# A two-block layer stack on one core: the second block's branch gates by seven products, as fillers of its attention

## The reference, cut to what matters

```python
proj = h @ w_in
(dq, dk, dv, sq, sk, sv, mq, mk, mv, g_diff, g_sb, g_moba) = jnp.split(proj, offsets, axis=-1)
...
merged = (jax.nn.sigmoid(g_diff) * (a_out @ w_diff_o)
          + jax.nn.sigmoid(g_sb) * (b_out @ w_sb_o)
          + jax.nn.sigmoid(g_moba) * (c_out @ w_moba_o))
return merged @ w_out
```

## Time and profile before

| | |
|---|---|
| median of 3 runs | 3370.44 us (3370.26 to 3370.8) |
| profiled execution | 3372.12 us, its span 3370.2 us |
| PE busy | 3293.4 us (98%), 22634 records |
| PEld busy | 2943.6 us (87%) |
| DVE busy | 2117.7 us (63%) |
| ACT busy | 683.3 us (20%) |
| POOL busy | 187.2 us (6%) |

### The profile page before, as it was taken

One profiled execution on the slowest core, in us unless ns is written; L12 is line 12 of the kernel. 1 busy time (PEld: TensorE's weight loads), 2 busy tenths in 40 slices (PEclk: granted clock), 3 DMA queues, 4 the chain that ended last, 5 costly groups with the idle time before them and its releaser, 6 DMA issues.

```text
span 3370.2 us, 54290 instructions
## 1 busy us (share of the span) xinstructions
PE 3293.4 (98%) x22634; PEld 2943.6 (87%) x22634; DVE 2117.7 (63%) x4269; ACT 683.3 (20%) x1675; POOL 187.2 (6%) x140
## 2 busy tenths in 40 slices
PE   7999999999999999999999999999999999999999
PEld 5888755788888888878999999987999999978999
DVE  3579554456554157765799685744586886644685
ACT  2101442012211011142122111124211212032211
POOL 0000000005443400000000000000000000000000
PEclk9999999999999999999999999999999999999999
DMA  6243001223223433403544445632444444633443
GB/s 235 81 174 127 26 26 63 96 85 128 87 86 111 147 152 129 175 35 113 199 179 168 169 163 176 175 138 100 147 169 169 163 165 159 193 115 121 155 163 126
DMA packets 67396, 453.76 MB, mean 135 GB/s; under 512 B 7376, under 2 KB 11856, under 8 KB 15056
## 3 DMA queue, kind: packets, MB, share of 16 engines
q1 hardware_dynamic: 66384, 446.09, 37.3%
q10 hardware_dynamic: 768, 4.20, 0.7%
HBM read 445.02 MB, written 1.05 MB: 132 GB/s over the span
## 4 chain that ended last, share of the span: by engine, by line
PE 88%; DVE 7%; ACT 2%; DMA 1%; issue 1%; SPq 0%; DVEq 0%; ACTq 0%
PE bank L1353 62%; PE bank L1041 14%; DVE conv_sum L2848 3%; PE bank L1667 2%; PE bank L1153 1%; PE bank L1183 1%; PE bank L1106 1%; PE bank L1091 1%; PE bank L1208 1%; PE bank L1714 1%; PE bank L1298 1%; DMA weight_ring<-w_o 1%; PE bank L1503 0%; PE bank L1276 0%; DMA weight_ring<-w_ada 0%
## 5 line engine op out<-in xcount | busy, mean ns | idle before, releaser
L1353 PE MATMUL bank<-normed,weight_ring 128*128 128x128 f32 (+1 forms) x5472 | 764.1, 295 | 5.3 <-ACT normed L1884 1.5
L1353 PEld LDWEIGHTS bank<-normed,weight_ring 128*128 128x128 f32 x5472 | 706.8, 192 | 42.5 <-issue 8.0
L1353 PE MATMUL bank<-normed,mixer_small 128*128 128x128 f32 (+1 forms) x3040 | 387.2, 281 | 0.0
L1353 PEld LDWEIGHTS bank<-normed,mixer_small 128*128 128x128 f32 x3040 | 366.4, 192 | 4.9
L1353 PE MATMUL bank<-region_a,weight_ring 128*128 128x128 f32 (+1 forms) x2128 | 294.4, 293 | 0.6 <-DVE region_a L2805 0.6
L1353 PEld LDWEIGHTS bank<-region_a,weight_ring 128*128 128x128 f32 x2128 | 272.1, 192 | 11.7 <-issue 2.0
L1353 PE MATMUL bank<-turned,weight_ring 128*128 128x256 f32 (+1 forms) x944 | 199.0, 353 | 0.0
L1353 PEld LDWEIGHTS bank<-turned,weight_ring 128*128 128x128 f32 x944 | 163.6, 190 | 18.4
L1041 PE MATMUL bank<-turned,weight_ring 128*128 128x256 f32 x768 | 179.5, 382 | 0.0
L1041 PEld LDWEIGHTS bank<-turned,weight_ring 128*128 128x128 f32 x768 | 140.8, 190 | 24.2 <-issue 6.9
L1353 PE MATMUL bank<-region_a,mixer_small 128*128 128x128 f32 (+1 forms) x1232 | 161.8, 282 | 0.0
(11 more groups left out here) (340 smaller groups left out, 4883.5 us busy)
## 6 DMA issues: line engine op xcount, KB each, us to landing
weight_ring<-w_ada SPq DMA_DIRECT2D x48, 1024.0 KB, 5.6
weight_ring<-w_up SPq DMA_DIRECT2D x44, 1024.0 KB, 4.8
weight_ring<-w_f1up SPq DMA_DIRECT2D x44, 1024.0 KB, 4.8
weight_ring<-w_f2up SPq DMA_DIRECT2D x44, 1024.0 KB, 4.8
weight_ring<-w_gt SPq DMA_DIRECT2D x32, 1024.0 KB, 4.8
weight_ring<-w_qk SPq DMA_DIRECT2D x24, 1024.0 KB, 4.8
weight_ring<-w_v SPq DMA_DIRECT2D x20, 1024.0 KB, 5.4
weight_ring<-w_pj SPq DMA_DIRECT2D x16, 1024.0 KB, 4.8
```

The costliest lines, as they stand in the source:

```text
L1353: mm = nc.tensor.matmul(bank[u.bank][:, pair.columns(p)], lhs(k), rhs(k), start=begins and p in pair.opens and k == 0, stop=ends and p in ...
```

## The change

The 24 gate tiles become 12 pairs, computed by the seven products. `GATE_PARTS` cuts a pair's products over its four filler halves: 1 and 2, then 7 and 6, in the even place; 5, then 3 and 4, in the odd place. Bank 6 holds y, bank 7 holds x. VectorE makes the four differences of the normed tokens ahead of the loop (into the free half of `normed`), the weight sums of pair j at n = 2j - 2 (`gate_sums`), and the mixes of tile n - 1 at n (`gate_mix`); the order in its loop at n is finish, scores, exponent, mix, sums (n even), store, squares. ScalarE copies only product 1 of a pair (`gate_first`, 128 columns). Sums have semaphores of their own (`gsums_made`, `gsums_used`); the second feed-forward part's first sums wait for the last of them.

```diff
+GATE_PARTS = [(1, 2), (7, 6), (5,), (3, 4)]
...
-                waited = 0 if 4 in order else 4
+                waited = had if had is not None else 0 if 4 in order else 4
...
+                    if name == "gt2":
+                        x = 2 * (g % 2) + half
+                        if g == 0 and half == 0:
+                            pe.wait_ge(turned_ready, T.next(turned_ready, 4))
+                        seven(b, g // 2 % SUM_RING, plan.pairs[name][g // 2], KD // 2, gate_act, gsums_made, gsums_used,
+                              True, True, l, wsum, None, None, GATE_PARTS[x], (0, 0, 3, 3)[x])
+                        return
...
-                    else:
-                        mm = product(bank[u.bank][:, 0:SEQ], b, g % 2 * KD + half * n, hnorm2, 0, SEQ, n, half * n,
-                                     half == 0, half == 1)
...
-                    a_(gates2[g // KD][:, g % KD, :], bank[u.bank][:, 0:SEQ], ACT.Copy).then_inc(bank_free[u.bank], 1)
+                    a_(one_gate[:, g // 2 % 2, :], bank[units[g].bank][:, 0:P], ACT.Copy).then_inc(one_copied, 1)
...
+                def gate_sums(j):
+                    ...
+                    if at_ >= SUM_RING:
+                        dve.wait_ge(gsums_used, at_ - SUM_RING + 1)
+                    dve.wait_ge(slot_landed[b.slot], (count(b, 0, l) + 1) * 16)
+                    ...
+                    v.tensor_tensor(s1, a21, a22, ALU.add).then_inc(gsums_made, 1)
+                    V.sent(gsums_made)
+                    v.tensor_tensor(a21, a11, a21, ALU.subtract).then_inc(gsums_made, 1)
+                    V.sent(gsums_made)
+                    dve.wait_ge(gsums_made, V.made["gsums_made"] - 1)
+                    v.tensor_tensor(s2, s1, a11, ALU.subtract).then_inc(gsums_made, 1)
+                    dve.wait_ge(gsums_made, V.at(gsums_made, V.sent(gsums_made)))
+                    v.tensor_tensor(s4, a12, s2, ALU.subtract).then_inc(gsums_made, 1)
+                    V.sent(gsums_made)
+
+                def gate_mix(n):
+                    ...
+                    if n % 2 == 0:
+                        mix_y(g // 2, y, gate_tiles(g), one_gate)
+                    else:
+                        mix_x(y, x, gate_tiles(g))
...
                     if 16 <= n + 1 < 24:
                         exponent(n + 1)
+                    gate_mix(n - 1)
+                    if n % 2 == 0:
+                        gate_sums(n // 2 + 1)
                     if n >= 1 and n % 2 == 0:
                         store(n // 2 - 1)
...
+                gate_mix(23)
                 store(11)
```

More of the change, by code:

```diff
@@ L272, in filler2 @@
         self.blocks[name][-1].after = self.units[name][-1]
+        if name == "gt2" and g % 2:
+            self.pairs.setdefault(name, []).append(Pair(self.units[name][-2:], P, False))
     def take_blocks(self, name, dram, n, cols, first=0):
@@ L1318, in attention1, with seven @@
                         turn(n + 1)
-            def seven(b, s, pair, n, act, made, used, begins, ends, l=0, ring=wsum, midway=None, behind_first=None, part=None):
+            def seven(b, s, pair, n, act, made, used, begins, ends, l=0, ring=wsum, midway=None, behind_first=None, part=None, had=None):
                 def quarter(q):
@@ L1677, in layer2 @@
                         value_part(u, b, t, range(KD)).then_inc(bank_full[u.bank], 1)
+                gate_act = Halves(hnorm2, lambda k: hn[:, k, 0:P], lambda k: hn[:, 4 + k, 0:P], lambda k: hn[:, k, P:2 * P],
+                                  0, KD // 2, 0, P, lambda what, k: None, lambda k: hn[:, 4 + k, P:2 * P])
                 def filler_half(i, half):
@@ L1686, in filler_half @@
                     n = KD // 2
-                    if name == "sv2":
-                        mm = value_part(u, b, g % 2, range(half * n, half * n + n))
-                    else:
-                        mm = product(bank[u.bank][:, 0:SEQ], b, g % 2 * KD + half * n, hnorm2, 0, SEQ, n, half * n,
-                                     half == 0, half == 1)
+                    mm = value_part(u, b, g % 2, range(half * n, half * n + n))
                     if half:
@@ L2882, in sums_of @@
                         dve.wait_ge(sums_used, V.next(sums_used))
+                    if x == FFN2:
+                        dve.wait_ge(gsums_used, (l + 1) * 12)
                     dve.wait_ge(slot_landed[b.slot], (count(b, 0, l) + 1) * 16)
@@ L3256, in halves, with mix_y @@
                     V.sent(turned_ready)
-                def mix_y(j, y, dst):
+                def mix_y(j, y, dst, one=one2):
                     dve.wait_ge(one_copied, V.next(one_copied))
@@ L3263, in mix_y @@
                     v.tensor_tensor(seg[:, 0:2], bank[y.bank][:, P:3 * P].rearrange("p (s c) -> p s c", c=P),
-                                    one2[:, j % 2, :].unsqueeze(1).to_broadcast([P, 2, P]), ALU.add).then_inc(mix_step, 1)
+                                    one[:, j % 2, :].unsqueeze(1).to_broadcast([P, 2, P]), ALU.add).then_inc(mix_step, 1)
                     dve.wait_ge(mix_step, V.at(mix_step, V.sent(mix_step)))
@@ L3446, in layer2 @@
                         dve.wait_ge(rope_ready, V.at(rope_ready, V.made["rope_ready"]))
+                n = KD // 2
+                b11, b21 = hnorm2[:, 0:n, 0:P], hnorm2[:, n:KD, 0:P]
+                b12, b22 = hnorm2[:, 0:n, P:2 * P], hnorm2[:, n:KD, P:2 * P]
+                dve.wait_ge(hnorm2_ready, (l + 1) * KD // 2)
+                v.tensor_tensor(hn[:, 0:n, 0:P], b12, b11, ALU.subtract).then_inc(turned_ready, 1)
+                dve.wait_ge(turned_ready, V.sent(turned_ready))
+                v.tensor_tensor(hn[:, n:KD, 0:P], b22, hn[:, 0:n, 0:P], ALU.subtract).then_inc(turned_ready, 1)
@@ new lines, in layer2, with gate_tiles @@
+                second = V.sent(turned_ready)
+                v.tensor_tensor(hn[:, n:KD, P:2 * P], b22, b12, ALU.subtract).then_inc(turned_ready, 1)
+                V.sent(turned_ready)
+                dve.wait_ge(turned_ready, second)
+                v.tensor_tensor(hn[:, 0:n, P:2 * P], b21, hn[:, n:KD, 0:P], ALU.subtract).then_inc(turned_ready, 1)
+                V.sent(turned_ready)
+                def gate_tiles(g):
+                    return gates2[g // KD][:, g % KD:g % KD + 2, :].rearrange("p a c -> p (a c)")
@@ new lines, in gate_sums @@
+                def gate_sums(j):
+                    if j >= 12:
+                        return
+                    b, at_ = plan.blocks["gt2"][j], 12 * l + j
+                    if j == 0:
+                        full_bank(plan.units["qk2"][-1], 0, l)
+                    if at_ >= SUM_RING:
+                        dve.wait_ge(gsums_used, at_ - SUM_RING + 1)
+                    dve.wait_ge(slot_landed[b.slot], (count(b, 0, l) + 1) * 16)
+                    a11, a12, a21, a22 = (ring_t[:, b.slot * SLOT + q * (KD // 2 * P):b.slot * SLOT + (q + 1) * (KD // 2 * P)] for q in range(4))
+                    s1, s2, s4 = (wsum[:, j % SUM_RING, i, 0:KD // 2 * P] for i in range(3))
+                    v.tensor_tensor(s1, a21, a22, ALU.add).then_inc(gsums_made, 1)
[7 more added lines that the diff above has]
+                    V.sent(gsums_made)
@@ L3448, in scores @@
+                def gate_mix(n):
+                    g = n if n % 2 == 0 else n - 1
+                    if not 0 <= g < 24:
+                        return
+                    y, x = plan.units["gt2"][g:g + 2]
+                    if n % 2 == 0:
+                        mix_y(g // 2, y, gate_tiles(g), one_gate)
+                    else:
+                        mix_x(y, x, gate_tiles(g))
                 def scores(n):
```

14 lines of the change are left out of this document (9 added, 5 removed).

## The result

The changed kernel takes 3405.93 us (median of five executions, 3399.0 to 3408.24) against 3370.44 us of five of the kernel before beside it (3365.01 to 3373.39): 1.0107 times, 95% interval 1.0093 to 1.012. The direction is the forecast's; the time is 12.5 us over it, at the upper edge of the range. The profiled execution took 3407.5 us, its span 3405.7.

What follows compares the result with a forecast made beforehand. TensorE was taken as the bound (88% of the chain of waits). New waits of +19.3 us a layer less a gain of 7.8 give +11.5, +23.0 over two layers: 3393.4 us from the median 3370.44, range 3374 to 3406.

Steps and rivals of the forecast that it cites:

- The gain: Gate products on TensorE: a pair goes from 6.91 to 6.25 us, saving 7.8 us a layer, 15.6 in all.
- The rule that weight loads set the pace: TensorE's gate records: loads alone would take a pair from 6.91 to 12.1 us, kernel some 3495 us; chance 0.01.
- The waits: TensorE waiting for VectorE's queue in the attention stage: 21.85 us a layer against 2.6 before, so +19.3.
- turn 8: TensorE's weight turn at n = 8, VectorE late from earlier periods: wait 2.2 us, bounds 0.8 and 3.6.
- turn 10: TensorE's weight turn at n = 10: VectorE's path 5.77 us against TensorE's 5.00, wait 0.8.
- norm sums at n = 10, 12: TensorE's norm sums, behind VectorE's sums, store and squares: 5.71 us against 4.01, wait 1.7, twice.
- turns 12, 14: TensorE's weight turns that waited 1.25 us for the norm's way through ScalarE: the half between shrinks, so 2.1, twice.
- turn 16: TensorE's weight turn at n = 16: VectorE's path 6.07 us against TensorE's 5.00, wait 1.05.
- turns 18, 20, 22 with product 5: TensorE's last three even-head turns: VectorE done 6.97 us after the odd turn against 3.66, wait 3.3, partly before product 5.
- the rival of a falling clock: TensorE's clock falls behind the new waits: six periods at 3.3 us each, kernel 3413 us; chance 0.04.
- TensorE stays the bound and the sums hide: Rival: VectorE's sums cost TensorE nothing in the attention stage, kernel 3354.8 us, faster; chance 0.08.
- Only the last stretch waits: Rival: VectorE catches up at n under 16, leaving 2.4 us a layer, kernel 3375.2, no measurable difference; chance 0.08.

Runs made afterwards that it cites:

- e8: Changed kernel with e5's order (mix before exponent, halves reordered, sums in odd places), each pair's sums one period earlier: 3358.3 us, ratio 0.9968.
- e9: Changed kernel with unused matmuls on TensorE ahead of turns 8, 12, 14, 16, 18, 20, 22 and the norm sums, 38 a layer: 3391.49 us, ratio 1.0068.
- e7: Changed kernel with six unused 256-column matmuls on TensorE ahead of each of the turns 18, 20 and 22: 3394.31 us, ratio 1.0085.
- e5: Changed kernel reordered: sums in odd places, mix before exponent, a pair's second half as products 3 and 4, then 5: 3361.86 us, ratio 0.9978.
- e1: Changed kernel without the gates' weight sums on VectorE, products taking raw weight blocks: 3366.52 us, ratio 0.9998.
- e2: Changed kernel with the same sums moved from even places behind the x mix to odd places behind the y mix: 3371.6 us, ratio 1.001.
- e3: Changed kernel with two of the four weight sums left in the even place and two moved to the odd: 3380.56 us, ratio 1.0029.
- e4: Kernel before, with five more VectorE instructions of 512 columns in each of places 16, 18 and 20: 3389.77 us, ratio 1.0069.

## Why the forecast was right in its waits and wrong in its time

**The gain** held. Sixteen records take 1.89 us with the change of kind (2305.70 to 2307.59 in the changed kernel; 1.79 + 0.1 forecast). In e8 the stage less its waits (3.85 us in six, each some 0.16 more from start to start, as 2310.60 + 0.99 to 2314.55 is 2.96 for a row of 2.79) is 117.1 us; before, 127.28 less 2.6 and twice 0.16 is 124.4. That is 7.3 a layer, the forecast 7.8. The rule that weight loads set the pace, which would have given 3495 us, does not hold here: PEld is busy 106.92 of 121.90 us in e8 and the records still keep their pace.

**The waits** held one by one. Forecast, then the row of layer 1 (a row lacks the 0.16):

| place | forecast | profiled idle |
|---|---|---|
| turn 8 | 2.2 | 1.99 |
| turn 10 | 0.8 | 0.70 |
| norm sums at n = 10, 12 | 1.7, 1.7 | 1.53, 1.54 |
| turns 12, 14 | 2.1, 2.1 | 2.09, 2.15 |
| turn 16 | 1.05 | 0.99 |
| turns 18, 20, 22 with product 5 | 3.3 each | 2.79 + 0.18 each |
| product 5 at n = 23 | 0.3 | 0.18 |

Turn 8's wait, the least certain of them, came the way that was forecast: from the second period on VectorE's sums start 8.93 us apart (2232.76, 2241.69, 2250.62), where 9.0 was forecast, against TensorE's 8.29 (8.3 forecast). e9 puts the waits in one number: 139.15 us where 138.8 was forecast.

**The step that failed** is the clock. The forecast took TensorE's clock as 1.00 in and behind the new waits, so its sum has no term for it, and gave the rival of a falling clock 0.04, with the reason that the kernel before's waits of 1.25 us left the stage's clock at 1.00. That row was about waits of 1.25 us and was carried to waits of 3.3 us. The clock did fall behind the long waits of both layers, for 7.8 us a layer (e9). The rival had the mechanism and the place, and was too dear: it priced six periods at 3.3 us each, where e7 gives 2.5; its 3413 against 3405.93. It should have had a larger part of the chance, or the forecast's own range a term of 0 to 20 us for it.

The trace of the kernel before could have said so. Its attention stages hold no wait over 1.31 us, but the first stack, of which the forecast uses one row near the start, holds longer ones. Two of them, each with a step of the busy table behind it:

```profile
255.68 2.89 PE L1353 MATMUL bank<-turned,region_a 128*128 128x256 f32 x8 [2.13 <-DVE region_a L2996]
258.00:260.00 2.00, 2.00 (x6) 1.62 (x5) 1.97 (x5) 0.00 (x0) 0.00 (x0) 0.50 0.00 0
...
1413.54 0.99 PE L1091 MATMUL bank<-region_b,constants 128*128 128x256 f32 x2 [1.90 <-DVE region_b L2734]
1414.00:1416.00 2.00, 2.00 (x6) 1.58 (x5) 1.43 (x5) 0.00 (x0) 0.00 (x0) 0.50 0.85 360
```

Behind waits of 2.13 and 1.90 us, shorter than those forecast for the last three turns, TensorE works at 0.50; behind others of that trace as long (1.96 us at 333, 1.92 at 1506) it stays at 1.00.

The sum then closes: 3393.2 for the span as forecast, 0.7 for the stages' own terms (2 x 0.35), 15.6 for the clock (2 x 7.8), 0.4 between the stages and -4.3 from the earlier start of the first stage give 3405.6; the span is 3405.7. That start is chance and not the change (in the ten traces it lies between 2209.82 and 2217.91): without it the miss would be larger. The clock's share differs from execution to execution too: the five lie between 3399.0 us, at a mean granted clock of 0.996, and 3408.24, at 0.992.

**The other rivals.** "TensorE stays the bound and the sums hide" fell for this order, and e5 and e8 show how near it is in another. Even without the sums (e1) it would not have come out, since the short half uncovers 2.1 us at turns 12 and 14. "Only the last stretch waits" fell at turns 8 and 10 and the norm sums.

**What stays open** is what decides whether the clock falls behind a given wait. The rows, as waits in the profiled executions: of 1.19 to 1.31 us at turns 12 and 14 (before, e5 and e8, both layers), none of twelve was followed by a fall; of 2.08 to 2.15 at the same turns in layer 1, none of two in the changed kernel, one of two in e1 and in e7, two of two in e2 and in e3; of 1.46 with 0.18 ahead in e3, two of three in either layer; of 2.77 in e4, one of six; of 2.79 with 0.18 ahead in the changed kernel, all six. Length alone does not order them. Nor does the program: the first stack is the same code in all ten kernels and holds a wait of 1.9 us near 1410 us and another near 1500 us. Behind the first the clock fell in four of the ten profiled executions, behind the second in seven. So whether a given wait brings a fall changes from execution to execution, and a forecast needs both ends. That idle time of TensorE is the cause of the late falls is shown by e7 and e9; which idle time suffices is not.

## What to carry to other kernels

Work put on a second engine is priced by what it stands in front of in that engine's queue: here the same products with the same sums are 35 us slower than the kernel before with the sums in one place, 3 us slower with them in another (e2), and 7 to 11 us faster when the mix and the halves are reordered too (e5, e8), at nearly the same busy time. Lay the queues of both engines end to end between two hand-overs, and put added work where the receiver has most of its own to do. When a forecast adds waits of TensorE, look through the whole trace for waits as long, read the granted clock in steps of a few us behind each, and price the half clock as a term with two ends, from no fall to a fall behind every wait.

## What the runs showed of the hardware

- Behind waits of 1.5 to 2.8 us between stretches of work TensorE's granted clock fell to 0.50, though not behind each of them, in the middle of kernels whose mean is 0.993 (the changed kernel, e3) to 0.997 (before, e2). In the changed kernel it stayed at 0.50 from the wait's end at 2314.55 until past 2320 (the 2 us from there are at 0.84). The Trainium skill (TensorE: Matmul & The Clock Gate, Part 1) has two clock levels, the lower one as the default, and activity as what releases it; the rows agree on the levels (0.50 and 1.00, with other values only over stretches that hold both) and on the release (back at 1.00 after work from 2314.55 to past 2320).
- The same kernel meets a different number of falls in different executions: e3's ten executions spread over 15.3 us, from 3370.63 at a mean granted clock of 0.997 to 3385.9 at 0.993; and one wait of 1.9 us near 1410 us, in code that all ten kernels share, was followed by a fall in four of ten profiles.
- Unused matmuls in TensorE's waits made a kernel faster: from 35.5 us over the kernel before to 26.2 over with 18 of them a layer (e7), and to 22.6 over with 38 (e9).
- fp32 records of 128 columns keep 0.112 us each with a weight load before each of them, also as fillers between other work (8 in 0.89 us, 2308.47 to 2309.36 in the changed kernel).
